# First feed-forward product of an encoder block with seven block products instead of eight, in six of eight groups

## The chip, the cores and the metric

One Trainium2 chip, of which the kernel uses 1 core. The metric is the device time of one launch in microseconds (us). Engines: TensorE (PE), VectorE (DVE), ScalarE (ACT), GpSimd (POOL) and SyncE (SP, which here only issues DMAs).

## What is computed

One layer of a residual block on x (1024 tokens x 1024, float32). What comes ahead of the feed-forward part (projections, chunked retention, stick-breaking attention, merge, output projection) is not touched. The feed-forward part is:

```
h2 = modulate(rmsnorm(h_res, pre_ffn_g), sh2, sc2)        # 1024 x 1024
f  = square(relu(h2 @ w_ff1)) @ w_ff2                     # w_ff1: 1024 x 4096, w_ff2: 4096 x 1024
h_res = h_res + gt2 * rmsnorm(f, post_ffn_g)
```

## The kernel before, in words

**Precision.** Every large product is made of two-part operands: a value is rounded to the PE's float32 format (`_hi`) and the rest is kept as a second part (`_lo`). A product is three matmuls into one PSUM bank (high by high, high by low, low by high): the triples at L549 to L551 and L933 to L935. ACT (sometimes DVE or POOL) makes the high part, DVE or POOL the low part.

**Groups.** The 4096 hidden columns are taken in 8 groups of 512 (`FF_G`). In each group PE first computes the hidden tiles, h2 times 512 columns of `w_ff1`, transposed: 8 tiles of 128 columns x 512 tokens (`ff_hidden`, 8 x 8 row chunks x 3 = 192 matmuls of 128x512). ACT takes ReLU and square of each tile into `hid` (L1259, L1261). Then comes the second product, `hid` times 512 rows of `w_ff2`, which is added to y. It is already a 2x2 block scheme with seven block products (P1, P4, P6, P5, P7, P3, P2 in the order of work, 7 x 24 = 168 matmuls, `product`); sums of the blocks a11, a12, a21, a22 of `hid` are made on DVE (L1782 to L1799), those of the blocks b11 to b22 of `w_ff2` on POOL (`add`, L487), the high parts on ACT (`w_high` L1248, `f_high` L1275), the low parts on DVE (`f_low`, L1763) and POOL (`low`, L487). DVE adds each finished bank into y (`evict`, L1776). Group 7 (`ff_last`) has no block scheme in its second product: 16 tiles x 12 matmuls (L975 to L977), with the final normalisation and the output rows behind each pair of tiles.

**Banks.** PSUM has eight banks: `pg` is banks 0 to 3, `px` banks 4 to 7. Hidden tiles use `pg` in turn; P1, P6, P7, P2 use `px`, the other three `pg`.

**Order.** Each engine runs one list of instructions in order and waits on semaphores; the order is written out by hand. Group 0 is unrolled, groups 1 to 6 are one loop, group 7 is unrolled. SP loads the weights in units of 512 KB, each when its buffer is free: four units of `w_ff1` through `raw` (2 slots), four of `w_ff2` into `w2`. The split token operands h2 stay in SBUF as `r_hi` and `r_lo` (64 KB a partition together) for all eight groups. Rounded weights have four slots in `w_hi` and `w_lo`.

Of the kernel before, what the change touches and what calls it, by code (L numbers as in the profile page):

```python
# [8 lines left out]
P = 128  # L9
D = 1024  # L10
# [120 lines left out]

class Steps:
# [19 lines left out]
def build_block(nc, x, wstream, ada, ada_rows, smalls, pos, ident, maskd, dprime, adab, postg, out, m1_dram, mods, x2_dram):  # L152
# [4 lines left out]
    with ctx:  # L157
# [86 lines left out]
        with ExitStack() as c:  # L244
            rh_f = sb("rh_f", [P, KC, S], f32, c)
            rl_f = sb("rl_f", [P, KC, S], f32, c)
# [7 lines left out]
        b11, b12, b21, b22 = (w2[:, b, :] for b in range(4))  # L254
        s2, t4 = hs[:, :, :], hs[:, :, :].rearrange("p a n -> p (a n)")
# [83 lines left out]
        gtg2_ready = sem("gtg2_ready")  # L339
        block = ctx.enter_context(nc.Block())  # L340
# [5 lines left out]
        def _(sp):  # L346
# [96 lines left out]
        def _(pool):  # L443
# [50 lines left out]
            def ff_group(g):  # L494
                first = isinstance(g, int)
                low(g, 4 + P1, 0, b11)
                pool.wait_ge(w2_in[1], 16 * g + 16)
                pool.wait_ge(ff_wlo, FF_UNITS * g + 4 + P1 + 1)
                add(b11, b12, b11, ALU.subtract).then_inc(ff_t, 1)
                if first:  # L500
# [4 lines left out]
                if not first:  # L505
# [1430 lines left out]
```

## Time and profile before

| | |
|---|---|
| time, median of 3 runs | 1748.8 us (1746.43 to 1750.7) |
| the profiled execution's own time | 1748.63 us |
| its span | 1746.8 us |
| mean granted TensorE clock | 0.995 |
| busy: PE, DVE, ACT, POOL | 1710.7, 904.0, 561.0, 603.5 us |
| moved by DMA over the span | 135.16 MB, mean 77 GB/s |

Busy time of PE counts matmuls whose ends are modelled, and one matmul's record overlaps the next. A row of a timeline gives start and duration; what stands in brackets is the idle time of the engine before it and what ended it. The share of the clock is the granted one, 1.00 being 2.4 GHz and 0.50 being 1.2 GHz.

### The profile page before, as it was taken

The page shows a single profiled execution, that of the slowest core. Times are in us where ns is not written, and L with a number is a line of the kernel's source. Part 1 is how long each engine was busy: PE and PEld are TensorE (multiplying, and loading weights), DVE is VectorE, ACT ScalarE, POOL GpSimd, SP SyncE. Part 2 cuts the span into 40 slices and gives each one's busy share as a digit, 9 for nine tenths or more (in the row PEclk, how much of TensorE's full clock was granted, in tenths as well). Part 3 has the DMA queues.
Part 4 walks back from the last instruction along what each step waited for, and adds up shares of the span by engine and source line. Part 5 has one row for each costly group of instructions (what it writes and reads, how often), then busy time and mean ns, then how long its engine had stood idle before and what let it go on. Part 6 is the DMA issues. An engine that isn't in the chain of part 4 may idle for free.

```text
span 1746.8 us, 25538 instructions
## 1 busy us (share of the span) xinstructions
PE 1710.7 (98%) x10016; PEld 1424.9 (82%) x10016; DVE 904.0 (52%) x1285; ACT 561.0 (32%) x952; POOL 603.5 (35%) x256
## 2 busy tenths in 40 slices
PE   5999999999999999999999999999999999999998
PEld 5877877777989898988888998788888888888876
DVE  6757676776446555652112277726261726252526
ACT  4556666210121212120002166333333333323242
POOL 1012111353323323233333742653535354444420
PEclk8999999999999999999999999999999999999999
DMA  8001001264401010113111545111111202020213
GB/s 341 25 25 50 17 33 61 85 217 169 148 25 52 25 53 31 46 37 133 48 48 48 175 164 193 48 49 51 46 60 36 72 24 72 24 85 12 71 66 127
DMA packets 38303, 135.16 MB, mean 77 GB/s; under 512 B 5956, under 2 KB 6852, under 8 KB 37704
## 3 DMA queue, kind: packets, MB, share of 16 engines
q1 hardware_dynamic: 30384, 109.66, 18.1%
q10 hardware_dynamic: 7832, 24.28, 3.7%
q8 instruction: 62, 1.02, 0.2%
q14 instruction: 25, 0.20, 0.0%
HBM read 121.33 MB, written 12.60 MB: 77 GB/s over the span
## 4 chain that ended last, share of the span: by engine, by line
PE 91%; DVE 4%; ACT 1%; DMA 1%; issue 1%; SPq 1%; POOL 0%; POOLq 0%; DVEq 0%; ACTq 0%
PE ps L551 17%; PE ps L549 17%; PE ps L550 17%; PE ps L933 5%; PE ps L935 5%; PE ps L934 5%; PE ps L636 3%; PE ps L637 3%; PE ps L638 3%; PE ps L812 2%; PE ps L689 2%; PE ps L814 2%; PE ps L813 2%; PE ps L653 1%; PE ps L671 1%; DMA ada_s<-ada 1%
## 5 line engine op out<-in xcount | busy, mean ns | idle before, releaser
L451 POOL TENSOR_TENSOR w_hi<-raw,zero 128x1024 fp32r<-128x1024 f32 x58 | 113.4, 1955 | 463.8 <-PE ps L551 279.9
L551 PE MATMUL ps<-r_hi,w_lo 128*128 128x512 f32 x640 | 254.3, 397 | 0.0
L549 PE MATMUL ps<-r_hi,w_hi 128*128 128x512 f32 x640 | 252.3, 394 | 0.0
L550 PE MATMUL ps<-r_lo,w_hi 128*128 128x512 f32 x640 | 252.0, 394 | 0.0
L549 PE MATMUL ps<-w_hi,a_hi 128*128 128x256 f32 x768 | 219.2, 285 | 0.8 <-DVE a_lo L1660 0.6
L551 PE MATMUL ps<-w_hi,a_lo 128*128 128x256 f32 x768 | 215.6, 281 | 0.0
L550 PE MATMUL ps<-w_lo,a_hi 128*128 128x256 f32 x768 | 215.3, 280 | 0.0
L487 POOL TENSOR_TENSOR w_lo<-w,w_hi 128x1024 fp32r<-128x1024 f32 x39 | 100.1, 2568 | 213.8 <-ACT w_hi L1248 213.8
L1776 DVE TENSOR_TENSOR m<-m,ps 128x512 f32<-128x512 f32 x208 | 136.6, 684 | 72.0 <-PE ps L935 71.5
L933 PE MATMUL ps<-w_hi,f_hi 128*128 128x512 f32 x392 | 155.5, 397 | 0.4 <-issue 0.4
L935 PE MATMUL ps<-w_hi,f_lo 128*128 128x512 f32 x392 | 155.4, 396 | 0.0
L934 PE MATMUL ps<-w_lo,f_hi 128*128 128x512 f32 x392 | 155.4, 396 | 0.0
L453 POOL TENSOR_TENSOR w_lo<-raw,w_hi 128x1024 fp32r<-128x1024 f32 x58 | 145.2, 2503 | 4.6
L549 PEld LDWEIGHTS ps<-w_hi,a_hi 128*128 128x128 f32 x768 | 144.8, 189 | 2.3 <-issue 0.9
L550 PEld LDWEIGHTS ps<-w_lo,a_hi 128*128 128x128 f32 x768 | 144.9, 189 | 0.2
L550 PEld LDWEIGHTS ps<-r_lo,w_hi 128*128 128x128 f32 x640 | 120.1, 188 | 30.3
L551 PEld LDWEIGHTS ps<-w_hi,a_lo 128*128 128x128 f32 x768 | 144.6, 188 | 0.0
L549 PEld LDWEIGHTS ps<-r_hi,w_hi 128*128 128x128 f32 x640 | 120.1, 188 | 28.9 <-DVE r_lo L1707 0.5
L551 PEld LDWEIGHTS ps<-r_hi,w_lo 128*128 128x128 f32 x640 | 120.1, 188 | 28.5
L1476 DVE TENSOR_TENSOR_SCAN uu<-uu 128x512 f32<-128x512 f32 (+7 forms) x96 | 96.1, 1041 | 77.3 <-ACT uu L1078 77.1
L1763 DVE TENSOR_TENSOR f_lo<-hid,f_hi 128x1024 fp32r<-128x1024 f32 x35 | 51.5, 1472 | 149.7 <-ACT f_hi L1275 149.7
L464 POOL TENSOR_TENSOR w_lo<-raw,w_hi 128x1024 fp32r<-128x1024 f32 x16 | 42.8, 2679 | 233.1 <-ACT w_hi L1000 205.2
(244 smaller groups left out, 3436.1 us busy)
## 6 DMA issues: line engine op xcount, KB each, us to landing
raw<-wstream SPq DMA_DIRECT2D x112, 512.0 KB, 3.6
ada_r<-ada_rows SPq DMA_DIRECT2D x32, 512.0 KB, 4.5
w<-wstream SPq DMA_DIRECT2D x32, 512.0 KB, 3.6
ada_s<-ada SPq DMA_DIRECT2D x7, 1024.0 KB, 17.1
m_dram<-m1s ACTq DMA_DIRECT2D x1, 4096.0 KB, 15.9
m<-m_dram ACTq DMA_DIRECT2D x1, 4096.0 KB, 13.0
x_dram<-m ACTq DMA_DIRECT2D x8, 512.0 KB, 5.1
rl_f<-x_dram ACTq DMA_DIRECT2D x2, 2048.0 KB, 9.4
```

What stands on the lines that cost most here:

```text
L451: nc.gpsimd.tensor_tensor(w_hi[:, slot, part], raw[:, h, :], zero[:, 0:1].broadcast_to([P, RAW]), ALU.add).then_inc(w_split, 1)
L453: nc.gpsimd.tensor_tensor(w_lo[:, slot, part], raw[:, h, :], w_hi[:, slot, part].bitcast(f32), ALU.subtract).then_inc(w_split, 1)
L487: return nc.gpsimd.tensor_tensor(out_, in0, in1, op)
L549: nc.tensor.matmul(outp, lh, rh, start=(k == 0), stop=False)
L550: nc.tensor.matmul(outp, lh, rl, start=False, stop=False)
L551: last = nc.tensor.matmul(outp, ll, rh, start=False, stop=(k == chunks - 1))
L636: nc.tensor.matmul(outp, hi, r_hi_, start=start, stop=False)
L933: nc.tensor.matmul(banks[:, t, :], fh, wh, start=(start and c == 0), stop=False, skip_group_check=not start)
L934: nc.tensor.matmul(banks[:, t, :], fh, wl, start=False, stop=False, skip_group_check=not start)
L935: last = nc.tensor.matmul(banks[:, t, :], fl, wh, start=False, stop=(c == 1), skip_group_check=not start)
L1476: V.tensor_tensor_scan(run, run, run, 1.0, ALU.mult, ALU.bypass).then_inc(scan_done, 1)
L1776: V.tensor_tensor(dst, dst, bank, op).then_inc(ff_ev, 1)
```

## The change

From the third group on (`FF_PLAIN = 2`) the hidden phase is a 2x2 block scheme as well. The blocks are the two halves of the 1024 rows of `w_ff1` (the sum's direction), the two halves of the tokens, and the two halves of the group's 512 columns. Seven products (Q1, Q2, Q6, Q7, Q5, Q4, Q3 in the order of work) of 2 banks x 4 chunks x 3 = 24 matmuls each take the place of 8 tiles of 24.

- The moving operands are seven: three are blocks of h2 (R11, R12, R22), four are sums of blocks (S1 to S4). They are the same in every group. SP stores the three in group 0 (6 DMAs of 1 MB). In group 1, DVE makes the four sums row block by row block (`operand_sums(k)`, k = 0 to 3, 13 instructions of 128x512 each), ACT rounds them (`sums_high(k)`, 4 instructions each), and SP stores both parts (16 DMAs of 512 KB). They go through slots 1 and 2 of `f_hi` and `f_lo`; a block's sums wait for the stores of the block before, and ACT's `f_high` of P4 and P6 waits for the last stores.
- `r_hi` and `r_lo` make room for a ring of three slots of 2 MB (`ring`) and four buffers for `w_ff1` (`w1s`). SP loads an operand into a slot as soon as the product that used the slot is done: seven loads of 2 MB per group.
- POOL makes the four sums of blocks of `w_ff1` and 7 low parts instead of 4; ACT makes 7 high parts instead of 4. With the second product this is 14 weight units a group instead of 11.
- The banks hold running sums: Q1, Q6 and Q7 accumulate in the same two banks, and ACT copies these out after each of the three (6 copies a group, `copied`); DVE adds the other banks to these copies in `hid` (8 additions, `h_sum`). Only then ACT takes ReLU and square, in place.
- The order of the second product stays. Group 1 is unrolled, groups 2 to 6 are the loop, group 7 takes its token tiles in the order 4 to 7, 0 to 3 (`LAST_T`) and loads the residual rows (`rl_f`) earlier.

The core of the diff:

```diff
+FF_PLAIN = 2
+Q1, Q2, Q6, Q7, Q5, Q4, Q3 = range(7)
+O_R11, O_R12, O_S2, O_S3, O_S1, O_R22, O_S4 = range(7)
+Q_WSLOT = (0, 1, 2, 3, 0, 1, 2)
+Q_RING = (0, 1, 2, 0, 1, 2, 0)
+P_WSLOT_W = (3, 0, 1, 2, 3, 0, 2)
+F_FREE_W = (8, 0, 4, 12, 16, 20, 24)
+W_UNITS, W_TILES, W_COPIES, W_ADDS, FF2_TILES = 14, 14, 6, 8, 28
+TL_W = TL_FF + FF_PLAIN * FF_TILES
+LAST_T = (4, 5, 6, 7, 0, 1, 2, 3)
...
+            ring = sb("ring", [P, 3, 2, 4, HALF], f32r, c)
+            w1s = sb("w1s", [P, 4, RAW], f32, c)
...
+            sp.wait_ge(n2_split, 32)
+            for o, k, th in ((O_R11, 0, 0), (O_R12, 4, 0), (O_R22, 4, 1)):
+                for part, a in enumerate((r_hi, r_lo)):
+                    sp.dma_start(ops[o, :, part, :, :], a[:, k:k + 4, th * HALF:(th + 1) * HALF].bitcast(f32)).then_inc(r_out, 16)
...
+            for k in range(4):
+                for pair, lo_done, to in ((0, 11, ops[O_S2:O_S3 + 1]), (1, 13, ops[O_S1:O_S4 + 1:2])):
+                    sp.wait_ge(s_val, 13 * k + lo_done)
+                    for part, f in enumerate((f_hi, f_lo)):
+                        sp.dma_start(to[:, :, part, k, :].rearrange("s p n -> p s n"), f[:, 1 + pair, :, :].bitcast(f32)).then_inc(s_out[pair], 16)
...
+            for o in range(3):
+                ring_load(o, gemm_done, TL_FF + FF_TILES + 8)
...
+            with sp.Fori(FF_PLAIN, FF_G - 1) as g:
+                wu = w_unit(g)
+                sp.wait_ge(w1_t, 4 * (g - FF_PLAIN) + 1)
+                w1_load(g + 1, 0, ff_wlo, wu + Q1 + 1)
+                ring_load(3, *h_done(g, 0))
+                ring_load(4, *h_done(g, 1))
+                ring_load(5, *h_done(g, 2))
+                w1_load(g + 1, 1, ff_wlo, wu + Q7 + 1)
+                ring_load(6, *h_done(g, 3))
+                ring_load(1, *h_done(g, 4))
+                w1_load(g + 1, 2, ff_wlo, wu + Q4 + 1)
+                ring_load(2, *h_done(g, 5))
+                ring_load(0, *h_done(g, 6))
+                w1_load(g + 1, 3, ff_wlo, wu + Q3 + 1)
...
+            def hidden_ahead(g, done):
+                n = 4 * (g - FF_PLAIN)
+                pool.wait_ge(ff_wlo, done)
+                if not isinstance(g, int) or g > FF_PLAIN:
+                    pool.wait_ge(w1_t, n)
+                for b in range(2):
+                    pool.wait_ge(w1_in[b], 16 * (g - 1))
+                add(u1, v12, v11, ALU.subtract).then_inc(w1_t, 1)
+                pool.wait_ge(w1_in[3], 16 * (g - 1))
+                pool.wait_ge(w1_t, n + 1)
+                add(u2, v22, u1, ALU.subtract).then_inc(w1_t, 1)
+                w_low(g, Q1, Q_WSLOT[Q1], v11)
+                w_low(g, Q2, Q_WSLOT[Q2], v21)
+            def hidden_units(g):
+                n = 4 * (g - FF_PLAIN)
+                w_low(g, Q6, Q_WSLOT[Q6], u2)
+                add(v12, v22, v12, ALU.subtract).then_inc(w1_t, 1)
+                w_low(g, Q7, Q_WSLOT[Q7], v12)
+                w_low(g, Q5, Q_WSLOT[Q5], u1)
+                pool.wait_ge(ff_wlo, w_unit(g) + Q2 + 1)
+                pool.wait_ge(w1_t, n + 2)
+                add(v21, u2, v21, ALU.subtract).then_inc(w1_t, 1)
+                w_low(g, Q4, Q_WSLOT[Q4], v21)
+                w_low(g, Q3, Q_WSLOT[Q3], v22)
...
+            def w_group(g):
+                wu = w_unit(g)
+                hidden_units(g)
+                w_low(g, 7 + P1, P_WSLOT_W[P1], b11)
+                second_sums(g, wu + 7 + P1 + 1)
+                w_low(g, 7 + P4, P_WSLOT_W[P4], t4)
+                w_low(g, 7 + P6, P_WSLOT_W[P6], t2)
+                w_low(g, 7 + P5, P_WSLOT_W[P5], b11)
...
+            def hidden_product(g, q, banks, start, free):
+                turn, slot = g - FF_PLAIN, Q_RING[q]
+                pe.wait_ge(ff_wlo, w_unit(g) + q + 1)
+                pe.wait_ge(ring_in[slot], (48 if slot == 0 else 32) * turn + 16 * (q // 3 + 1))
+                for m in range(2):
+                    pe.wait_ge(*free(m))
+                    for k in range(4):
+                        wh, wl = (w[:, Q_WSLOT[q], k * 256 + m * P:k * 256 + (m + 1) * P] for w in (w_hi4, w_lo4))
+                        xh, xl = (ring[:, slot, part, k, :] for part in range(2))
+                        nc.tensor.matmul(banks[:, m, :], wh, xh, start=(start and k == 0), stop=False, skip_group_check=not start)
+                        nc.tensor.matmul(banks[:, m, :], wl, xh, start=False, stop=False, skip_group_check=not start)
+                        last = nc.tensor.matmul(banks[:, m, :], wh, xl, start=False, stop=(k == 3), skip_group_check=not start)
+                    last.then_inc(h_mm, 1)
+            def hidden_products(g):
+                turn, ev = g - FF_PLAIN, FF_EVS * (g - 1)
+                x_banks, z_banks, y_banks, w_banks = px[:, 0:2, :], px[:, 2:4, :], pg[:, 0:2, :], pg[:, 2:4, :]
+                hidden_product(g, Q1, x_banks, True, lambda m: (ff_ev, ev + E_P2 + m + 1))
+                hidden_product(g, Q2, z_banks, True, lambda m: (ff_ev, ev + E_P2 + m + 3))
+                hidden_product(g, Q6, x_banks, False, lambda m: (h_copy, W_COPIES * turn + m + 1))
+                hidden_product(g, Q7, x_banks, False, lambda m: (h_copy, W_COPIES * turn + m + 3))
+                hidden_product(g, Q5, y_banks, True, lambda m: (ff_ev, ev + E_P3 + m + 1))
+                hidden_product(g, Q4, w_banks, True, lambda m: (ff_ev, ev + E_P3 + m + 3))
+                hidden_product(g, Q3, y_banks, False, lambda m: (h_add, W_ADDS * turn + m + 3))
...
+            def sums_high(k):
+                for n, ready in ((1, 3), (0, 5), (2, 8), (3, 9)):
+                    act.wait_ge(s_val, 13 * k + ready)
+                    nc.scalar.activation(f_hi[:, 1 + n // 2, n % 2, :], sum_slot(n), ACT.Copy).then_inc(s_hi, 1)
...
+                    if j == 0 and not first:
+                        sums_high(0)
...
+                    if j == 2 and not first:
+                        sums_high(1)
...
+                    sums_high(2)
...
+                    sums_high(3)
...
+                else:
+                    act.wait_ge(s_out[0], 16 * 8)
...
+                else:
+                    act.wait_ge(s_out[1], 16 * 8)
...
+            def hidden_part(g, seconds):
+                turn, tl, t1 = g - FF_PLAIN, w_tiles(g), 4 * (g - FF_PLAIN)
+                def h(q):
+                    return h_mm, W_TILES * turn + 2 * q + 2
+                act.wait_ge(ff_lo, FF_PRODS * g)
+                unit_high(Q_WSLOT[Q6], u2, (gemm_done, tl + 8), (w1_t, t1 + 2))
+                copied(g, 0, 0, 0, px[:, 0, :])
+                unit_high(Q_WSLOT[Q7], v12, (gemm_done, tl), (w1_t, t1 + 3))
+                copied(g, 1, 1, 0, px[:, 1, :])
+                unit_high(Q_WSLOT[Q5], u1, h(Q1), (w1_t, t1 + 1))
+                squared(g, 0, 0, 0)
+                squared(g, 1, 1, 0)
+                f_high_w(g, P1, a11, ff_sq, 8 * g + 2)
+                unit_high(Q_WSLOT[Q4], v21, h(Q2), (w1_t, t1 + 4))
+                copied(g, 2, 2, 0, px[:, 0, :])
+                copied(g, 3, 3, 0, px[:, 1, :])
+                unit_high(Q_WSLOT[Q3], v22, h(Q6), (w1_in[3], 16 * (g - 1)))
+                copied(g, 4, 0, 1, px[:, 0, :])
+                copied(g, 5, 1, 1, px[:, 1, :])
+                unit_high(*seconds[0])
+                squared(g, 2, 2, 1)
+                squared(g, 3, 3, 1)
+                unit_high(*seconds[1])
+                f_high_w(g, P4, a22, ff_sq, 8 * g + 4)
+                squared(g, 4, 0, 1)
+                squared(g, 5, 1, 1)
+                unit_high(*seconds[2])
...
+            def operand_sums(k):
+                def s_(f, n):
+                    return f[:, 1 + n // 2, n % 2, :]
+                def step(n, out_, in0, in1, op, after):
+                    if after:
+                        dve.wait_ge(s_val, 13 * k + after)
+                    V.tensor_tensor(out_, in0, in1, op).then_inc(s_val, 1)
+                (h11, l11), (h21, l21), (h12, l12), (h22, l22) = (
+                    tuple(r[:, c, th * HALF:(th + 1) * HALF].bitcast(f32) for r in (r_hi, r_lo))
+                    for c, th in ((k, 0), (k, 1), (4 + k, 0), (4 + k, 1)))
+                x2_, x3, x1, x4 = (sum_slot(n) for n in range(4))
+                tmp = fs_f[:, 1, HALF:D]
+                if k:
+                    dve.wait_ge(s_out[0], 32 * k)
+                else:
+                    dve.wait_ge(gemm_done, TL_FF + 28)
+                step(1, x3, h11, h21, ALU.subtract, 0)
+                step(2, tmp, l11, l21, ALU.subtract, 0)
+                step(3, x3, x3, tmp, ALU.add, 2)
+                step(4, x2_, h22, x3, ALU.subtract, 3)
+                step(5, x2_, x2_, l22, ALU.add, 4)
+                if k:
+                    dve.wait_ge(s_out[1], 32 * k)
+                else:
+                    dve.wait_ge(gemm_done, TL_FF + 32)
+                step(6, x1, x2_, h11, ALU.add, 5)
+                step(7, x4, h12, x2_, ALU.subtract, 0)
+                step(8, x1, x1, l11, ALU.add, 6)
+                step(9, x4, x4, l12, ALU.add, 7)
+                for m, n in enumerate((1, 0, 2, 3)):
+                    dve.wait_ge(s_hi, 4 * k + m + 1)
+                    step(10 + m, s_(f_lo, n), sum_slot(n), s_(f_hi, n).bitcast(f32), ALU.subtract, 9 if m == 0 else 0)
...
+                    for k in range(3):
+                        operand_sums(k)
...
+                else:
+                    operand_sums(3)
...
+            def hidden_sums(g):
+                for m in range(2):
+                    h_sum(g, m, half(m, 0), half(m, 0), px[:, 2 + m, :], ALU.add, 1 + m)
+                f_low_w(g, 0, 0, a11)
+                for m in range(2):
+                    h_sum(g, 2 + m, half(2 + m, 1), half(m, 1), pg[:, m, :], ALU.add, 5 + m)
+                f_low_w(g, 1, 1, a22)
+                for m in range(2):
+                    h_sum(g, 4 + m, half(m, 1), half(m, 1), pg[:, 2 + m, :], ALU.subtract, 5 + m)
```

## Rows read from the trace of the kernel before

**Rows 1.** The page: busy time, and shares of the chain that ended last.
```profile
PE 1710.7 (98%) x10016; PEld 1424.9 (82%) x10016; DVE 904.0 (52%) x1285; ACT 561.0 (32%) x952; POOL 603.5 (35%) x256
...
PE 91%; DVE 4%; ACT 1%; DMA 1%; issue 1%; SPq 1%; POOL 0%; POOLq 0%; DVEq 0%; ACTq 0%
```

**Rows 2.** The waits of PE: total us, times, longest (first and seventh of 12).
```profile
PE ps L601 <- DMA ada_s<-ada: 17.9, 1, 17.9
...
PE ps L975 <- POOL w_lo L487: 0.7, 1, 0.7
```

**Rows 3.** Groups by line on PE: busy us, mean ns.
```profile
L551 PE MATMUL ps<-r_hi,w_lo 128*128 128x512 f32 x640 | 254.3, 397 | 0.0
L549 PE MATMUL ps<-r_hi,w_hi 128*128 128x512 f32 x640 | 252.3, 394 | 0.0
```

**Rows 4.** Timeline of PE: first matmul of group 1 and of group 2.
```profile
1144.07 0.39 PE L549 MATMUL ps<-r_hi,w_hi 128*128 128x512 f32 x1
...
1228.21 0.40 PE L549 MATMUL ps<-r_hi,w_hi 128*128 128x512 f32 x1
```

**Rows 5.** Window of group 1's hidden phase: busy PE, PEld, DVE, ACT, POOL; clock, DMA, GB/s.
```profile
1144.00:1189.00 45.00, 45.00 (x194) 36.20 (x194) 10.07 (x7) 16.77 (x22) 22.50 (x9) 1.00 0.09 33
```

**Rows 6.** DVE on two SBUF tensors (line L1652): min/median/max ns.
```profile
L1652 DVE TENSOR_TENSOR m<-m,gate x16: 691/693/2841, 812.8 to 962.3; 128x512 f32 x12, 128x512 f32<-128x512 f32 x4
```

**Rows 7.** DMA issues: KB each, us to landing; whole span, and three short windows.
```profile
w<-wstream SPq DMA_DIRECT2D x32, 512.0 KB, 3.6
...
x_dram<-m ACTq DMA_DIRECT2D x8, 512.0 KB, 5.1
...
x_dram<-m ACTq DMA_DIRECT2D x1, 512.0 KB, 9.1
...
rl_f<-x_dram ACTq DMA_DIRECT2D x1, 2048.0 KB, 7.2
...
rl_f<-x_dram ACTq DMA_DIRECT2D x2, 2048.0 KB, 9.4
```

**Rows 8.** Timeline of DVE and of POOL in group 1, the same stretch.
```profile
1169.05 2.08 DVE L1763 TENSOR_TENSOR f_lo<-hid,f_hi 128x1024 fp32r<-128x1024 f32 x1 [24.10 <-ACT f_hi L1275]
1171.05 3.41 DVE L1782 TENSOR_TENSOR hid<-hid 128x1024 f32<-128x1024 f32 x1
...
1167.63 2.42 POOL L487 TENSOR_TENSOR w<-w 128x1024 f32<-128x1024 f32 x1
1170.04 3.34 POOL L487 TENSOR_TENSOR w_lo<-hs,w_hi 128x1024 fp32r<-128x1024 f32 x1
```

**Rows 9.** Groups by line on ACT from 1140 on: busy us, mean ns.
```profile
L1248 ACT ACTIVATE w_hi<-w 128x1024 fp32r<-128x1024 f32 x34 | 35.5, 1044 | 0.0
L1261 ACT ACTIVATE hid<-hid 128x512 f32<-128x512 f32 x56 | 35.4, 633 | 1.8
L1259 ACT ACTIVATE hid<-ps 128x512 f32<-128x512 f32 x56 | 33.5, 598 | 186.1 <-PE ps L551 186.1
```

**Rows 10.** Timeline of DVE: the low part of a22 in group 1.
```profile
1186.10 1.22 DVE L1763 TENSOR_TENSOR f_lo<-hid,f_hi 128x1024 fp32r<-128x1024 f32 x1
```

**Rows 11.** Windows around PE's stop of 1.9 us; the clock is third from last.
```profile
96.00:97.00 1.00, 0.00 (x0) 0.00 (x0) 0.05 (x1) 1.00 (x4) 1.00 (x1) 1.00 0.00 0
...
98.00:99.00 1.00, 1.00 (x4) 0.75 (x4) 0.79 (x3) 0.00 (x0) 0.00 (x0) 0.64 0.35 70
99.00:100.00 1.00, 1.00 (x4) 0.81 (x3) 0.00 (x0) 0.00 (x0) 0.00 (x0) 0.50 0.85 279
100.00:101.00 1.00, 1.00 (x3) 0.72 (x3) 0.00 (x0) 0.00 (x0) 0.00 (x0) 0.50 0.42 168
101.00:102.00 1.00, 1.00 (x4) 0.84 (x3) 0.00 (x0) 0.00 (x0) 0.00 (x0) 0.65 0.02 8
```

**Rows 12.** Window while two loads of 2048 KB are under way; GB/s is last.
```profile
1703.00:1705.00 2.00, 2.00 (x10) 1.58 (x10) 1.71 (x3) 0.00 (x0) 0.00 (x0) 1.00 1.07 459
```

More of the change, by code:

```diff
@@ new lines, in _, with w1_load, ring_load @@
+            for c in range(2):
+                load(unit(1, c), c, (ff_wlo, 2 + c + 1))
+            for b, p in ((0, P5), (1, P7), (3, P3), (2, P2)):
+                ff_second(1, b, (ff_wlo, 4 + p + 1))
+            for c in range(2, 4):
+                load(unit(1, c), c - 2, (ff_wlo, FF_UNITS + c - 1))
+            def w1_load(g, b, *after):
+                sp.wait_ge(*after)
+                sp.dma_start(w1[b], unit(g, b)).then_inc(w1_in[b], 16)
+            def ring_load(o, *after):
+                sp.wait_ge(*after)
+                sp.dma_start(ring[:, Q_RING[o], :, :, :].bitcast(f32), ops[o, :, :, :, :]).then_inc(ring_in[Q_RING[o]], 16)
@@ L922, in ff_hidden, with passes_t, product @@
                             h2_transposed(u)
-            def product(g, i, banks, start, free):
-                pe.wait_ge(ff_wlo, FF_UNITS * g + 4 + i + 1)
+            def passes_t(bank, hidden, weight, start, stop, skip):
+                (fh, fl), (wh, wl) = hidden, weight
+                nc.tensor.matmul(bank, fh, wh, start=start, stop=False, skip_group_check=skip)
+                nc.tensor.matmul(bank, fh, wl, start=False, stop=False, skip_group_check=skip)
+                return nc.tensor.matmul(bank, fl, wh, start=False, stop=stop, skip_group_check=skip)
+            def product(g, i, banks, start, free, unit, slot):
+                pe.wait_ge(ff_wlo, unit + i + 1)
                 pe.wait_ge(ff_lo, FF_PRODS * g + i + 1)
@@ new lines, in unit_high, with hidden_ahead @@
+            def unit_high(slot, src, free, ready):
+                act.wait_ge(*ready)
+                act.wait_ge(*free)
+                nc.scalar.activation(w_hi4[:, slot, :], src, ACT.Copy).then_inc(ff_whi, 1)
+            def hidden_ahead(g):
+                end = w_tiles(g) + 8
+                unit_high(Q_WSLOT[Q1], v11, (gemm_done, end - 4), (w1_in[0], 16 * (g - 1)))
+                unit_high(Q_WSLOT[Q2], v21, (gemm_done, end - 4 if isinstance(g, int) else end - 16), (w1_in[2], 16 * (g - 1)))
@@ L1776, in evict @@
                     V.tensor_tensor(dst, dst, bank, op).then_inc(ff_ev, 1)
+                if not first:
+                    for k in range(3):
+                        operand_sums(k)
                 f_low(P1, a11)
@@ L1817, in ff_group, with h_sum @@
                 dve.wait_ge(ff_ev, ev + FF_EVS)
[L1819 to L1824 removed]
+            def h_sum(g, n, dst, src, bank, op, copy):
+                turn = g - FF_PLAIN
+                dve.wait_ge(h_mm, W_TILES * turn + (3, 4, 9, 10, 11, 12, 13, 14)[n])
+                dve.wait_ge(h_copy, W_COPIES * turn + copy)
+                V.tensor_tensor(dst, src, bank, op).then_inc(h_add, 1)
```

372 lines of the change are left out of this document (248 added, 124 removed).

## The prediction, made before the changed kernel was built or run

> **What bounds the kernel now.** I read the page first. TensorE (PE) is busy 98% of the span and makes 91% of the chain that ended last [rows 1]. The list of its waits says the same: the one long wait is for the first inputs, and within the feed-forward stage only the last group shows one, 0.7 us [rows 2]. So in the groups that the change touches, PE never waits, and the stage costs its matmuls. A matmul's printed duration (394 to 397 ns, the same at each of the three places of a triple) is no price, since they overlap [rows 3]. The price is the distance of starts: the first matmul of group 1 starts at 1144.07 and that of group 2 at 1228.21, with 360 matmuls of 128x512 between them, so one costs 84.14/360 = 0.2337 us [rows 4]. 24 of them, now one hidden tile and in the new scheme one product, cost 5.61 us. DVE is busy 10.1 us of the 45 of group 1's hidden phase, ACT 16.8 and POOL 22.5 [rows 5]; all three have room, and the question is whether the change fills it in the wrong place.
>
> **What is removed.** In groups 2 to 7 the hidden phase goes from 8 tiles x 24 = 192 matmuls to 7 products x 24 = 168. The bound engine loses 24 x 0.2337 = 5.61 us per group, 33.7 us for six. The order inside a triple becomes high-high, low-high, high-low; I cost it at nothing, because the three places have the same mean today. Everything else the change does is added work, which costs nothing while it lies beside PE.
>
> **Added once: the operands, in group 1.** Six stores of 1 MB of the token operands go out on SP's queue at the end of the split in group 0. Behind them on SP wait only loads for group 1, needed a group later: nothing. Then DVE makes four sums for each of four row blocks, 13 steps of 128x512 each, 52 in all, ACT rounds 16 of them, and 16 stores take them to DRAM. These are a chain. A block's step 1 overwrites what the block before is still storing, so it waits for that block's first pair of stores, issued after step 11. And DVE stands in order: the low part of a11 (needed by P1) is behind block 2, the low part of a22 (needed by P4) behind block 3 and, through ACT, behind block 3's stores.
> Prices: a DVE step between SBUF tensors lasts 0.69 us, some 0.65 per step where they follow closely, so 11 steps 7.2 us [rows 6]. A 512 KB store has landed after 5.1 us, and a pair after some 5.5 us with the second issue [rows 7]. DVE and POOL hold each other up: DVE's low part started at 1169.05 and took 2.08 us, and the next operation 3.41, while POOL's operations ran 1167.63 to 1170.05 and then 3.34 us instead of 2.42; the two take turns [rows 8].
> In time from the group's first matmul: ACT can round only after ReLU and square of the first tile, 5.61 + 1.23 = 6.9 [rows 9], and the first block's step 11 is over at about 12.4. Its stores have landed at 17.9. Block 1 takes 7.2 plus three POOL operations that come between (weight sums and lows, 3 x 2.4): 32.3. Stores 37.8; block 2 to 45.0; two steps and the low part of a11 to 47.4, while P1 wants it at 8 x 5.61 = 44.9. Block 2's stores 50.5; block 3 to 57.7; its stores 63.2; ACT's copy 64.3; the low part of a22 at 65.5. P4 wants it at 50.5 (today it is there at 1187.3, 43.2 after the start [rows 10]). That is 15.0 us late, and 1 us more while evictions catch up: **16 us**. Bounds: 1 us, if blocks never hold P4 (DVE has 35 idle us in this phase); 30 us, if each of the four store pairs takes the 9.1 us that one store took in a busy moment.
> After a stop of 1.9 us (PE has no instruction from 96 to 97) the granted clock stood at 0.64, 0.50, 0.50 and 0.65 for the next four microseconds, that is at the lower of the two levels (1.2 GHz) for most of it: 1.7 us lost [rows 11]. I add 1.7 for the long stop; bounds 0 and 3.4 (two stops).
>
> **Added in every group from 2 on.** ACT gets 6 copies from PSUM and 3 weight roundings (about 6.5 us), DVE 8 additions with a PSUM operand (5.5 us), POOL 7 operations (17 us) [rows 6, 8, 9]. Against a group of 336 x 0.2337 = 78.5 us that is room enough, so only order matters. I laid the steps against products of 5.61 us. Weights of Q6 high, low 3.5; POOL's sum 5.9; Q7 high 7.0, low 9.4; Q5 low 11.8; the next sum 14.3; ACT, in order, rounds Q4's weights to 15.3 and only then copies Q6's first bank, 15.9; Q7 wants that bank at 16.8: 0.9 us to spare. Further on POOL's four sums end at 36.3, DVE's low part of a22 stands behind them, then sums, ReLU, square and the evictions of P1: P4 has 1.5 us to spare, P6 some 1.9, and P5's first bank 0.4 us. No stop, but margins of under a microsecond; I take 0.1 us per group, bounds 0 and 2.5. In the last group the low part of a21 is about 1.0 us late, while the wait of 0.7 us there today goes, since its weights have 4.2 us of matmuls over them and need 3.6 [rows 2]: +0.3. Together 0.8 us.
> The ring: seven loads of 2 MB per group, on SP. A load is issued when its slot's product ends and is wanted two products, 11.2 us, later. A 2048 KB load of the same shape landed after 7.2 us, the second issued 0.4 us behind it after 11.7 (the median of both is 9.4), so 4.9 us each when they follow [rows 7]. Four such loads and one of 0.5 MB (8.9 MB) are wanted between the end of Q1 and the start of Q3, with 25.8 us for the transfers: 346 GB/s. A window of a loaded queue shows 459 GB/s [rows 12]. So the ring holds with about 4 us to spare: nothing. The Trainium skill (DMA: Bandwidth & Descriptors, Specifications) gives an HBM limit near 358 GB/s per core; by that the spare would be 0.9 us and the sum the same. By the 341 GB/s that its section Bandwidth gives for 1 MB each group would stop 0.3 us and the sum be 2 us more. This trace's window stands above both figures.
>
> **Sum**, against the profiled execution's own time of 1748.6 (span 1746.8; the median of three runs is 1748.8): 1748.6 - 33.7 + 16.0 + 1.7 + 0.8 = **1733.4 us**. The 0.2 between that execution and the median is left aside.
>
> **Rivals.**
> B, group 1 hides its sums, and nearly all of the saving is kept. For it: DVE is idle 35 of 45 us there, and ACT 28. Against: the chain of four blocks and stores above is 57 us long and has only 50.5. 1748.6 - 33.7 + 1 + 0.8 = 1716.7.
> C, the groups of the loop stop as well, in P5's or Q7's bank wait: each margin is under 1 us, and one more blocked POOL operation (3.34 - 2.42 = 0.9 us, [rows 8]) in each of two chains eats it. 2.5 us per loop group, five of them: 1733.4 + 12.5 = 1745.9, from 1737 to 1750.
> D, the other side: **slower**, by the ring. If loads on the queue do not overlap and each takes its 7.2 us [rows 7], then four of them and the 512 KB load (3.6 us) end at 5.6 + 32.4 = 38.0 and Q3, which wants the last at 33.7, stops 4.3 to 5 us in each group: 1733.4 + 6 x 4.7 = 1761.6. It decides from about 6.9 us per load. Against: the two loads that did overlap.
> E, the products save nothing, since weights of 256 columns and the ring as moving operand cost more per matmul: 1733.4 + 33.7 = 1767.1. Against: rows 3, one price for all operands.
>
> **Chances.** Forecast 0.60, B 0.15, C 0.14, D 0.07, E 0.04. A measurement of this kernel can tell about 0.2%, 3.5 us, from no change. Forecast and B are faster, and of C two thirds (below 1745.3): faster 0.84. The rest of C and the upper end of the forecast: same 0.07. D and E: slower 0.09 with rounding. The range takes in B's 1716 below, and above the group-1 bound and most of C, 1748; D and E are left out.
>
> **What would show it.** Right: PE's waits in the profile of after name DVE's low part for the first matmul of P4, once, with 10 to 15 us, and of P1 with about 2; group 1 takes about 100 us instead of 84.1, each loop group 78.5 to 79; the granted clock falls once, behind that stop. Wrong: no such wait (B); waits for evictions or ACT's copies five times over (C); waits for the DMA into the ring (D); a start distance above 0.234 us in the products (E).

## The result, and the profile after

The changed kernel takes 1759.4 us (median of four runs, 1756.1 to 1766.1) against 1749.8 for the kernel before beside it: the ratio is 1.0064, with a 95% interval of 1.0047 to 1.0082. It is slower by 0.6%. The prediction had said 1733.4 us, between 1716 and 1748, and faster with a chance of 0.84. It was wrong in its sign.

The page of the changed kernel begins with the busy times; the profiled execution took 1756.1 us:

```profile
span 1754.3 us, 25638 instructions
...
PE 1686.2 (96%) x9872; PEld 1401.3 (80%) x9872; DVE 995.2 (57%) x1385; ACT 606.4 (35%) x1022; POOL 711.5 (41%) x298
...
PE 70%; POOL 10%; issue 9%; DVE 5%; ACT 3%; DMA 2%; SPq 0%; DVEq 0%; POOLq 0%; ACTq 0%
```

Beside [rows 1] TensorE's (PE's) share falls from 98% to 96% of a longer span, and in the chain that ended last from 91% to 70%. Ten per cent of that chain are now GpSimd (POOL), five VectorE (DVE). PE does less work and waits for others. Its waits, with the total, the number and the longest in us:

```profile
PE ps L1074 <- DVE m L2193: 14.0, 5, 2.8
PE ps L1074 <- issue: 14.0, 4, 7.9
PE ps L1074 <- DVE hid L2163: 4.7, 5, 1.0
```

The kernel before had none of these ([rows 2]). Two of them come five times, once in each group of the loop (groups 2 to 6): 0.84 to 0.98 us ahead of P4's first matmul, for VectorE's last hidden sums, and 2.8 us ahead of P5's, for VectorE's evictions of P4's banks. The two lines of "DVE" are the loop's; the line of "issue" holds the stops of 2.65 and 7.88 us in group 1, the last group's of 3.04, and one of 0.39 that the kernel before has too. The timeline of PE shows the loop's and the two stops of group 1; a row has start, duration, line, operation, and in brackets the idle time before it and what ended it:

```profile
1189.13 0.77 PE L1074 MATMUL ps<-w_hi,f_hi 128*128 128x512 f32 x1 [2.65 <-issue]
...
1205.64 0.77 PE L1074 MATMUL ps<-w_hi,f_hi 128*128 128x512 f32 x1 [7.88 <-issue]
...
1286.85 0.51 PE L1074 MATMUL ps<-w_hi,f_hi 128*128 128x512 f32 x1 [0.84 <-DVE hid L2163]
...
1301.15 0.80 PE L1074 MATMUL ps<-w_hi,f_hi 128*128 128x512 f32 x1 [2.78 <-DVE m L2193]
1301.74 0.63 PE L1075 MATMUL ps<-w_lo,f_hi 128*128 128x512 f32 x1
1302.17 0.63 PE L1076 MATMUL ps<-w_hi,f_lo 128*128 128x512 f32 x1
```

The last two rows start 0.43 us apart in place of 0.23: that is the lower clock level (1.2 GHz) behind a stop. By stage, with the window, its length, the busy time and count of PE, PEld, DVE, ACT and POOL, then the granted clock, the DMA share and GB/s. The rows are group 1's hidden and second products, group 2's, group 4's, and the last group's hidden products:

```profile
1141.51:1189.13 47.62, 44.97 (x194) 35.88 (x192) 39.70 (x41) 20.41 (x30) 21.05 (x8) 0.99 0.35 128
1189.13:1240.95 51.82, 43.94 (x168) 34.92 (x169) 42.70 (x54) 16.95 (x21) 22.80 (x9) 0.87 0.65 255
1240.95:1280.24 39.29, 39.29 (x169) 31.45 (x168) 7.15 (x9) 18.59 (x25) 32.03 (x14) 1.00 0.84 337
1280.24:1325.24 45.00, 41.38 (x170) 32.65 (x168) 38.46 (x42) 15.59 (x19) 23.32 (x10) 0.96 0.33 127
1409.62:1448.82 39.20, 39.20 (x170) 31.53 (x168) 7.15 (x9) 18.43 (x25) 31.84 (x14) 1.00 0.84 333
1448.82:1492.48 43.66, 39.87 (x169) 31.48 (x168) 37.69 (x42) 15.73 (x19) 23.50 (x10) 1.00 0.35 132
1659.68:1702.09 42.41, 39.37 (x169) 31.38 (x168) 11.07 (x11) 22.65 (x30) 25.49 (x12) 1.00 0.60 229
```

What the reader is to see:
- Group 1 takes 47.62 + 51.82 = 99.4 us in place of 84.1 [rows 4]: +15.3.
- The seven hidden products take 39.2 us, 0.2333 us per matmul, with PE busy all the time while the ring is loaded at 337 GB/s. That stage saves its 5.6 us in full.
- The second products behind them take 43.7 to 45.0 us, where 168 matmuls without a stop need 39.3. The saving goes there: loop groups take 82.8 to 84.4 us, 83.7 in the mean (418.7 us from 1240.95 to 1659.68 for five), against 84.1 before.
- The last group stops for 3.04 us ahead of its second products.
- A stop costs more than the time in its brackets: the brackets count from the end of the last matmul's record, 0.39 us long, where the next would have started after 0.23, and the first start behind a stop is followed late. Experiment 1 gives the price of one alone: 1.2 us for 0.98 in brackets.

Over the whole span, from 1746.8 to 1754.3 us: group 1 begins 2.6 us earlier here than in the profile of before, and takes 15.3 more; the five loop groups take 418.7 - 5 x 84.14 = -2.0; what is left behind them takes 94.6 in place of 1746.8 - (1228.21 + 5 x 84.14) = 97.9, so -3.3. The sum is +7.4.

### The profile page after: what moved, and what is told of

The parts are those of the page before. It is cut to its first block, busy times and chain, and to the rows that moved or that the text cites. A ratio compares the mean times of both kernels' runs of the same rounds, so it can differ in the third digit from the quotient of the medians.

```text
span 1754.3 us, 25638 instructions
## 1 busy us (share of the span) xinstructions
PE 1686.2 (96%) x9872; PEld 1401.3 (80%) x9872; DVE 995.2 (57%) x1385; ACT 606.4 (35%) x1022; POOL 711.5 (41%) x298
## 4 chain that ended last, share of the span: by engine, by line
PE 70%; POOL 10%; issue 9%; DVE 5%; ACT 3%; DMA 2%; SPq 0%; DVEq 0%; POOLq 0%; ACTq 0%
PE ps L696 12%; PE ps L698 11%; PE ps L697 11%; POOL w_lo L578 5%; PE ps L1074 3%; PE ps L1075 3%; PE ps L1076 3%; PE ps L783 3%; PE ps L784 3%; PE ps L785 3%; PE ps L959 2%; POOL w1s L578 2%; PE ps L836 2%; PE ps L961 2%; PE ps L960 2%
## 5 line engine op out<-in xcount | busy, mean ns | idle before, releaser
L1074 PE MATMUL ps<-w_hi,f_hi 128*128 128x512 f32 x440 | 179.7, 408 | 32.7 <-DVE m L2193 14.0
L1075 PE MATMUL ps<-w_lo,f_hi 128*128 128x512 f32 x440 | 178.0, 405 | 0.0
L1076 PE MATMUL ps<-w_hi,f_lo 128*128 128x512 f32 x440 | 177.5, 403 | 0.0
L1119 PE MATMUL ps<-ring,w_hi 128*128 128x512 f32 x336 | 133.1, 396 | 0.0
L1117 PE MATMUL ps<-ring,w_hi 128*128 128x512 f32 x336 | 132.7, 395 | 0.0
L1118 PE MATMUL ps<-ring,w_lo 128*128 128x512 f32 x336 | 132.5, 394 | 0.0
L1074 PEld LDWEIGHTS ps<-w_hi,f_hi 128*128 128x128 f32 x440 | 85.2, 194 | 59.1 <-DVE m L2193 16.2
L2193 DVE TENSOR_TENSOR m<-m,ps 128x512 f32<-128x512 f32 x160 | 99.9, 678 | 15.0 <-PE ps L1076 14.3
L2163 DVE TENSOR_TENSOR hid<-hid,ps 128x512 f32<-128x512 f32 x48 | 31.8, 681 | 129.4 <-PE ps L1119 129.4
L1076 PEld LDWEIGHTS ps<-w_hi,f_lo 128*128 128x128 f32 x440 | 85.2, 194 | 21.0
L696 PE MATMUL ps<-r_hi,w_hi 128*128 128x512 f32 x256 | 101.9, 398 | 0.1
```

The source lines that it names most:

```text
L696: nc.tensor.matmul(outp, lh, rh, start=(k == 0), stop=False)
L1074: nc.tensor.matmul(bank, fh, wh, start=start, stop=False, skip_group_check=skip)
L1075: nc.tensor.matmul(bank, fh, wl, start=False, stop=False, skip_group_check=skip)
L1076: return nc.tensor.matmul(bank, fl, wh, start=False, stop=stop, skip_group_check=skip)
L1117: nc.tensor.matmul(banks[:, m, :], wh, xh, start=(start and k == 0), stop=False, skip_group_check=not start)
L1118: nc.tensor.matmul(banks[:, m, :], wl, xh, start=False, stop=False, skip_group_check=not start)
```

## Why VectorE was late: the theory before the runs

The timeline of VectorE in group 2's second products:

```profile
1281.64 1.22 DVE L2197 TENSOR_TENSOR hid<-hid 128x1024 f32<-128x1024 f32 x1 [1.95 <-ACT hid L1556]
1282.90 3.30 DVE L2200 TENSOR_TENSOR hs<-hid 128x1024 f32<-128x1024 f32 x1
1286.12 1.27 DVE L2163 TENSOR_TENSOR hid<-hid,ps 128x512 f32<-128x512 f32 x2
...
1291.39 2.48 DVE L2193 TENSOR_TENSOR m<-m,ps 128x512 f32<-128x512 f32 x4
1293.78 3.40 DVE L2208 TENSOR_TENSOR hs<-hid,hs 128x1024 f32<-128x1024 f32 x1
1297.11 3.38 DVE L2172 TENSOR_TENSOR f_lo<-hid,f_hi 128x1024 fp32r<-128x1024 f32 x1
1300.42 2.47 DVE L2193 TENSOR_TENSOR m<-m,ps 128x512 f32<-128x512 f32 x4
```

and of GpSimd in the same stretch:

```profile
1282.64 2.48 POOL L578 TENSOR_TENSOR w_lo<-gate,w_hi 128x1024 fp32r<-128x1024 f32 x1 [1.86 <-ACT w_hi L1535]
1291.29 8.12 POOL L578 TENSOR_TENSOR w_lo<-w,w_hi 128x1024 fp32r<-128x1024 f32 x3 [6.17 <-ACT w_hi L1535]
```

A VectorE operation of 128x1024 between SBUF operands takes 1.22 us when it is left alone. Three here take 3.3 to 3.4, each beside a GpSimd operation (a "meeting" in what follows). L2200 became ready 0.26 us after GpSimd had begun the low part of P6's weights (1282.64); the sums that free P4's banks (L2163) stand behind it, and P4 stopped. In the same way L2208 and L2172 each lost 2.2 us to the second and third low part of GpSimd's row of three (P5's, P7's, P3's); the evictions that free P5's first banks stand behind them, and P5 stopped for 2.8 us. The evictions themselves, with an operand in PSUM, kept their 0.62 us each beside the first. L2200, L2208 and the L2172 behind it take 3.29 to 3.43 us in every group of the loop. P7's and P3's weights are wanted only 5.6 and 11.2 us after P5's.

So **the theory**: GpSimd's low parts, made earlier than needed, take VectorE's turns on SBUF. The Trainium skill (SBUF — State Buffer, Who interferes with whom) says that such a pair of operations goes by an exclusive lock held for a whole instruction, and that the issue order decides who blocks. The rows agree: the 3.40 us of L2208 are 2.2 of waiting behind a GpSimd operation that had begun and the 1.22 of its own.

**Rivals**: VectorE's list alone is too long, whoever runs beside it; ScalarE's high parts, which moved with GpSimd's, are in the way; the ring's loads slow the others. For group 1 the theory is the forecast's chain of sums and stores. The page names only "issue" for its two stops, but VectorE's low parts of a11 and of a22 end just ahead of the two rows of PE above, at 1189.03 (PE: 1189.13) and 1205.55 (1205.64):

```profile
1187.81 1.22 DVE L2097 TENSOR_TENSOR f_lo<-hid,f_hi 128x1024 fp32r<-128x1024 f32 x1
...
1204.32 1.23 DVE L2097 TENSOR_TENSOR f_lo<-hid,f_hi 128x1024 fp32r<-128x1024 f32 x1 [1.64 <-ACT f_hi L1478]
```

## The experiments

All ratios are against the kernel before, on the same chip in the same batch. "Less than the changed kernel" compares medians of different batches, in which the kernel before took 1749.8 (changed kernel), 1749.3 (experiments 1, 3, 4 and 5) and 1748.5 us (2, 6 and 7); differences of one or two microseconds in it say nothing.

**1. GpSimd's low parts of P7 and P3 later.**

```diff
-                unit_high(*second(P7, b12, (gemm_done, tl + 12), ff_t, 4 * g + 4))
+                unit_high(*second(P7, b12, (gemm_done, tl + 18), ff_t, 4 * g + 4))
...
-                unit_high(*second(P3, b22, (gemm_done, tl + 16), w2_in[3], 16 * g + 16))
+                unit_high(*second(P3, b22, (gemm_done, tl + 22), w2_in[3], 16 * g + 16))
```

> Only ScalarE's gates of the high parts of P7's and P3's weights move six tiles of the second products later, so that GpSimd does their low parts later; the instructions and their sizes stay the same. Theory (VectorE and GpSimd take turns on SBUF, and GpSimd's lows of P7 and P3 hold up VectorE's sum for a12 and the low part of P5's hidden operand): the stop of 2.8 us ahead of P5's first matmul goes, and the half clock behind it; the stop of 0.84 to 1.0 us ahead of P4 stays. Loop groups 79.5 to 80.7 us instead of 83.7, in all 15 to 22 us less than the changed kernel: about 1739 us. Rival (VectorE has too much to do between P1 and P5, whatever GpSimd does): P5's stop stays at 2.8 us, and the time at 1757 to 1760. Rival (the ring's loads hold the matmuls up): no change either.

Measured: 1739.7 us, ratio 0.9953 (0.9936 to 0.9970), 19.7 us less than the changed kernel. The waits of PE in the feed-forward stage:

```profile
PE ps L1074 <- issue: 15.5, 4, 9.1
PE ps L1074 <- DVE hid L2163: 4.8, 5, 1.0
```

The five stops of 2.8 us are gone, and the clock falls in no loop group; each takes 79.8 us (39.2 and 40.6), as expected; the five together take 398.9 in place of 418.7. P4's stop stays, as the theory said. It is now alone in its stage, so its price can be read: 0.98 us in brackets, and 40.59 us against the 39.35 of a stage without a stop.

```profile
1282.40:1322.99 40.59, 39.61 (x169) 31.56 (x168) 34.56 (x42) 15.85 (x19) 23.33 (x10) 1.00 0.38 143
```

Two numbers in two lines of ScalarE's list turn the change from a loss into a gain.

**2. GpSimd alone later.** The first experiment moved ScalarE's work too. Here ScalarE keeps its times.

```diff
+                pool.wait_ge(gemm_done, w_tiles(g) + 18)
                 w_low(g, 7 + P7, P_WSLOT_W[P7], b12)
+                pool.wait_ge(gemm_done, w_tiles(g) + 22)
                 w_low(g, 7 + P3, P_WSLOT_W[P3], b22)
```

> As in the first experiment, but ScalarE keeps its times: only GpSimd waits, ahead of its lows of P7 and P3, for the tiles of the second products that ScalarE waited for there. Theory (it is GpSimd's turns on SBUF that hold VectorE up): the stop of 2.8 us ahead of P5 goes as in the first experiment, loop groups 79.8 us, time 1738 to 1742 us. Rival (the moved work of ScalarE was the cause, its high parts in VectorE's way): the stop stays, 1755 us or more.

Measured: 1740.3 us, ratio 0.9951 (0.9939 to 0.9964), the same as the first. VectorE's timeline at the same place of group 2:

```profile
1293.90 2.47 DVE L2195 TENSOR_TENSOR m<-m,ps 128x512 f32<-128x512 f32 x4
1296.29 1.22 DVE L2210 TENSOR_TENSOR hs<-hid,hs 128x1024 f32<-128x1024 f32 x1
1297.42 1.22 DVE L2174 TENSOR_TENSOR f_lo<-hid,f_hi 128x1024 fp32r<-128x1024 f32 x1
1298.56 2.47 DVE L2195 TENSOR_TENSOR m<-m,ps 128x512 f32<-128x512 f32 x4
```

The same instructions in the same order; the two behind the first evictions take 1.22 us in place of 3.40 and 3.38. For P5's stop, VectorE's list is not too long and ScalarE is not the cause: it is GpSimd's turns.

**3. The hidden sums first.** VectorE makes the sums that free P4's banks ahead of the two subtractions.

```diff
                 hidden_sums(g)
+                for m in range(2):
+                    h_sum(g, 6 + m, half(2 + m, 0), half(2 + m, 0), pg[:, m, :], ALU.add, 3 + m)
                 dve.wait_ge(ff_sq, 8 * g + 6)
...
-                for m in range(2):
-                    h_sum(g, 6 + m, half(2 + m, 0), half(2 + m, 0), pg[:, m, :], ALU.add, 3 + m)
                 f_low_w(g, P6, P_FSLOT[P6], s2)
```

> Only VectorE's order changes: the last two sums of the hidden tile (numbers 6 and 7, which free P4's banks) come ahead of the two subtractions that form a11 - a21 and s2. Theory: the stop of 0.84 to 1.0 us ahead of P4 goes in each of the five loop groups, and the stop ahead of P5 shrinks by up to 0.8 us because VectorE's list shifts; 4 to 9 us less than the changed kernel, about 1752 us. Rival (work amount of VectorE alone sets both stops): the 0.9 us only moves to P5's stop, time as before this edit, 1757 to 1760.

Measured: 1752.7 us, ratio 1.0019 (1.0006 to 1.0031), 6.8 us less than the changed kernel, within the 4 to 9 expected. In the profile the loop's five groups take 408.7 us in place of 418.7.

```profile
PE ps L1074 <- issue: 15.5, 4, 9.1
PE ps L1074 <- DVE m L2193: 11.8, 5, 2.4
```

P4's stop is gone and P5's fell from 2.8 to 2.4 us. The 0.9 us did not move on to P5: the rival of pure work amount fails here as well. That P4's stop itself comes from a meeting is worked out and not tested: L2200 loses 2.1 us to GpSimd's low part of P6's weights, more than the stop of 0.84 to 0.98, but no run took that meeting away. What this run shows is that the order of VectorE's list decides.

**4. Both orders, and the last group's.** To both edits comes one in the last group: ScalarE makes the high part of a21 ahead of the third weight unit's.

```diff
                 squared(g, 5, 1, 1)
+                if isinstance(g, int):
+                    act.wait_ge(ff_sq, 8 * g + 6)
+                    act.wait_ge(gemm_done, w_tiles(g) + 4)
+                    nc.scalar.activation(f_hi[:, 2, :, :], a21, ACT.Copy).then_inc(ff_hi, 1)
                 unit_high(*seconds[2])
```

> Both edits together, and in the last group ScalarE makes the high part of a21 ahead of the high part of the third weight unit. Theory: no stop over 0.3 us in any loop group, each 78.5 to 79 us; the last group's stop of 3.0 us falls to 1 us or less; group 1 stays at 99.4 us. In all 25 to 29 us less than the changed kernel: about 1731 us, that is 18 us below the kernel before. Rival (work amount): loop groups stay above 82 us and the time above 1752 us.

Measured: 1731.0 us, ratio 0.9902 (0.9885 to 0.9919), 28.4 us less than the changed kernel. By stage: group 1's second products, group 2's hidden and second products, the last group's hidden products:

```profile
1191.23:1243.95 52.72, 43.59 (x169) 34.59 (x170) 43.60 (x54) 16.95 (x21) 22.90 (x9) 0.87 0.64 250
1243.95:1283.15 39.20, 39.20 (x169) 31.55 (x168) 7.57 (x10) 18.43 (x25) 31.93 (x14) 1.00 0.85 338
1283.15:1322.51 39.36, 39.36 (x169) 31.65 (x168) 34.73 (x42) 15.86 (x19) 23.33 (x10) 1.00 0.39 146
1636.69:1676.98 40.29, 39.37 (x169) 31.38 (x168) 9.76 (x11) 22.23 (x30) 22.32 (x11) 1.00 0.58 217
```

A loop group is 39.20 + 39.36 = 78.6 us, 336 matmuls at 0.234: PE without a stop, and the full 5.6 us saved in each. The last group's stop is 0.9 us; with either order alone it was still 3.0 (experiments 1 and 3), so it is the third edit that shortened it. VectorE's subtraction that forms s2 is still blocked (3.31 us); the sums that P4 waits for no longer stand behind it, so it costs nothing.

**5. No operand sums.** Left out: the 52 operand sums of group 1 with their 16 high parts and 16 stores; the ring's four slots of sums are filled from operands that are in DRAM anyway.

```diff
-                    for k in range(3):
-                        operand_sums(k)
...
-                    operand_sums(3)
...
-                sp.dma_start(ring[:, Q_RING[o], :, :, :].bitcast(f32), ops[o, :, :, :, :]).then_inc(ring_in[Q_RING[o]], 16)
+                sp.dma_start(ring[:, Q_RING[o], :, :, :].bitcast(f32), ops[(O_R11, O_R12, O_R11, O_R22, O_R12, O_R22, O_R11)[o], :, :, :, :]).then_inc(ring_in[Q_RING[o]], 16)
```

> Left out: the 52 operand sums of group 1 with their ScalarE high parts and their 16 stores; the ring's four slots of sums are filled from three operands that are in DRAM anyway, so traffic and matmuls stay the same. Theory: group 1's stops of 2.65 and 7.9 us and the half clock behind each go, group 1 falls from 99.4 to 84.1 us, everything behind stays: 15 to 16 us less than the changed kernel, about 1744 us. Rival (the stops of group 1 come from loads or from GpSimd's own work): group 1 stays above 92 us, time above 1751 us.

Measured: 1747.3 us, ratio 0.9986 (0.9974 to 0.9997). Group 1, hidden and second products:

```profile
1148.30:1193.10 44.80, 44.80 (x194) 36.04 (x193) 10.58 (x7) 16.77 (x22) 22.50 (x9) 1.00 0.09 32
1193.10:1232.44 39.34, 39.34 (x169) 31.64 (x168) 26.79 (x37) 11.28 (x12) 20.26 (x8) 1.00 0.61 243
```

44.80 + 39.34 = 84.1 us without a stop: the sums and stores are all of group 1's 15.3, and the rival falls. The time is a miss: the median fell by 12.2 us and not by 15 to 16. Between the two profiled executions it is 8.5, that is 15.3 less in group 1 and 6.8 more ahead of it, where no instruction was edited (group 1 begins at 1148.30 here and at 1141.51 in the changed kernel's). The loop's groups keep their stops and their 418.7 us.

**6. The ring's traffic.** Left out: nearly all bytes of the loop's ring loads (16 partitions by 16 columns of each row in place of 2 MB); waits and counts are kept.

```diff
-                sp.dma_start(ring[:, Q_RING[o], :, :, :].bitcast(f32), ops[o, :, :, :, :]).then_inc(ring_in[Q_RING[o]], 16)
+                sp.dma_start(ring[0:16, Q_RING[o], :, :, 0:16].bitcast(f32), ops[o, 0:16, :, :, 0:16]).then_inc(ring_in[Q_RING[o]], 16)
```

> Left out: nearly all of the ring's traffic. In the loop each of the seven loads into the ring moves 16 partitions by 16 columns of each row in place of 2 MB, so 35 loads of 2 MB go; the matmuls read what the ring held before, waits and counts are the same. Theory: the ring's loads cost nothing in the changed kernel, since the hidden stage runs at 0.2333 us per matmul with no stop: the time stays at 1757 to 1761 us. Rival (the loads' traffic slows VectorE and GpSimd in SBUF or lengthens the weights' landings, and so makes the stops): loop groups below 82 us and the time below 1750 us.

Measured: 1762.5 us, ratio 1.0079 (1.0065 to 1.0092), 3 us above the changed kernel and 1.5 above the bound given. Its waits:

```profile
PE ps L1079 <- issue: 16.8, 4, 10.7
PE ps L1079 <- DVE m L2198: 14.0, 5, 2.8
PE ps L1079 <- DVE hid L2168: 5.0, 5, 1.0
```

The loop's stops are what they were with 35 loads of 2 MB beside them, and its five groups take 419.0 us against 418.7 (1245.98 to 1664.93). The ring costs nothing. It was close, though. In the changed kernel's group 2 a load takes up to 10.9 us from its issue to its landing (first row: minimum, median, maximum), where 11.2 are allowed: the one issued at 1263.54 was there at 1274.43, and Q3, which reads it, began at 1274.55. For 25 us the loads moved 396 GB/s at a DMA share of 0.98 (second row):

```profile
DMA to landing us min/median/max: 8.4/10.2/10.9
```

```profile
1249.00:1274.40 25.40, 25.40 (x111) 20.34 (x109) 3.98 (x5) 11.99 (x17) 20.18 (x9) 1.00 0.98 396
```

Whether the 3 us are more than noise is open (the intervals of the two ratios overlap); they are not in the loop. The two profiled executions lie 8.1 us apart: 4.1 ahead of group 1; 1.0 in group 1's second products (52.8 us against 51.8), which were not edited; 0.2 in the loop; and 2.8 behind the last group's stop, where the clock falls, which it didn't in the changed kernel (26.8 us against 24.0 for the next 102 matmuls).

**7. The sums in two groups.** On top of experiment 4, group 2 keeps eight products as well, the seven begin in group 3, and the four blocks of sums are made two in group 1 and two in group 2; the loads, counts and gates of group 2 follow those of group 1.

```diff
-FF_PLAIN = 2
+FF_PLAIN = 3
...
-                    for k in range(3):
+                    for k in (2 * g - 2, 2 * g - 1):
                         operand_sums(k)
...
-                    operand_sums(3)
```

> On top of both orders: group 2 too keeps its eight products, the seven products begin in group 3, and the operand sums are made half in group 1 and half in group 2. It gives up 24 matmuls (5.6 us) and should be rid of group 1's stops (99.4 us against 84.1 us without the sums). Theory (only the length of VectorE's list ahead of the low part of a11 and of a22 makes these stops, and two blocks are done some 33 us into a group, 15 us ahead of P1): groups 1 and 2 take 84.1 to 84.5 us each, the loop groups 78.6 us, in all 9 to 10 us less than with both orders in place: about 1721 us, 28 us below the kernel before. Rival (the stops come with the sums wherever they stand, in proportion): groups 1 and 2 take some 91 us each and the time is 1735 us or more.

Measured: 1725.1 us, ratio 0.9850 (0.9834 to 0.9866). It is 1.5% faster than the kernel before. By stage: group 1, group 2, then the first group with seven products:

```profile
1148.80:1193.60 44.80, 44.80 (x194) 36.04 (x193) 38.86 (x33) 21.33 (x30) 23.77 (x9) 1.00 0.35 126
1193.60:1232.94 39.34, 39.34 (x169) 31.64 (x168) 27.05 (x37) 11.39 (x12) 15.24 (x6) 1.00 0.22 72
1232.94:1277.74 44.80, 44.80 (x193) 36.04 (x192) 38.73 (x33) 21.33 (x30) 23.26 (x9) 1.00 0.35 125
1277.74:1317.09 39.35, 39.35 (x169) 31.64 (x168) 27.24 (x37) 11.28 (x12) 20.30 (x8) 1.00 0.61 243
1317.09:1356.29 39.20, 39.20 (x170) 31.54 (x168) 7.57 (x10) 18.47 (x25) 31.93 (x14) 1.00 0.86 341
1356.29:1395.64 39.35, 39.35 (x170) 31.64 (x168) 34.70 (x42) 15.85 (x19) 23.30 (x10) 1.00 0.39 143
```

VectorE is busy 38.9 of 44.8 us in the hidden phase, nearly as in the changed kernel (39.7), and PE does not stop once in groups 1 to 6: the same sums are free where only two blocks stand ahead of the low part of a11. The second block is done 34.1 us into the group, 10.7 ahead of P1 (the expectation's 15 was not right). The size came out 4 us short of the expected 1721: two of the five runs took 1720, three 1725 to 1726, and in the profiled one, of the latter three, group 1 begins 5.2 us later than in experiment 4. From there to the end it takes 575.5 us against 586.1, so 10.6 less where 9 to 10 were expected.

## Why the prediction was wrong, step by step

- **The removed matmuls, 33.7 us: right.** Per group 5.61 us; experiment 4 shows 84.14 - 78.56 = 5.6 in each loop group. Rival E falls.
- **The ring, nothing: right.** No wait for it in any profile, 39.2 us per hidden stage at 337 GB/s, and none of the stops went with the traffic in experiment 6. But the spare was not the 4 us of the forecast. The last load that group 2 needed was there 0.1 us before Q3 began (experiment 6), so the term came out right by little. Rival D, the only one on the slower side beside E, falls, though the kernel is slower.
- **Group 1, 16.0 and 1.7 us: right.** Sum 17.7, measured 15.3, shown by experiment 5 (15.3 to 16.3 in the six profiles that have all sums in group 1). The forecast had the low part of a22 at 65.5 us after the group's start; it came at 1204.32 + 1.23 - 1141.51 = 64.0. The third block's stores were forecast at 45.0 and issued at 45.2 (1186.71). The stops are 2.65 and 7.9 us where 2 and 10 to 15 were named. P4's first matmul came 64.1 us after the start, 13.6 later than the 50.5 at which it was wanted, where 15.0 were forecast; another 1.7 us went behind it, where 1.0 and 1.7 had been set. Nineteen matmuls ran at the lower clock (3.7 us), but 13 of them between the two stops, where P4 waited for VectorE anyhow. The clock fell behind both stops and again in the loop, not once. Rival B falls.
- **A price inside that chain was short.** Six steps of the first two blocks met a GpSimd operation and took 2.8 to 2.9 us in place of 0.69, four of them in the second block (8.5 us, where the forecast set 7.2 for three GpSimd operations). How much of group 1's 15.3 us would go if GpSimd's weight sums stood elsewhere was not tried.
- **The loop groups: the step that failed.** "No stop, but margins of under a microsecond; I take 0.1 us per group, bounds 0 and 2.5" was 5.2 us per group (83.7 - 78.5), 26 us in all. It is nearly the whole miss. In the profiled execution, 1756.1 us, the parts are: 25.5 more in the loop (26 where 0.5 was set), 2.4 less in group 1, 2.0 more in the last group (0.3 forecast, 2.3 measured: 3.04 in place of 0.7), and 2.6 less ahead of group 1, so 1733.4 + 22.5 = 1755.9. That 1733.4 + 26 also gives the median, 1759.4, is chance.
- **What was wrong inside that step.** The step let VectorE's operations take their free time and named no GpSimd low part beside them on the way to P4 and P5. Rival C had the sign right, waits for evictions in the five loop groups, but its price of 2.5 came from one blocked GpSimd operation (0.9 us) in each of two chains. It read the turn-taking of [rows 8] from GpSimd's side. From VectorE's side the same rows say 3.41 where 1.22 is free: 2.2 us per meeting, and VectorE is the engine in the chain. Three of its operations meet one in each group, 3.30, 3.40 and 3.38 us, 6.4 us against margins of 1.5 and 0.4. The two stops make 3.7 us of the 5.2 per group visible, and cost some 0.25 us each beyond their brackets; the lower clock behind P5's adds 1.5 us in three of five groups, 0.9 in the mean.
- **The chances.** The margins of 0.4 to 1.9 us were written down beside a price per meeting of 2.2 that could be read from the rows. With margins smaller than one meeting, the loop stopping was the likely case and not one of 0.14, and its upper bound belonged at three meetings per group, above the kernel before.
- **What would show it.** The text named "waits for evictions or ACT's copies five times over" as the sign of C. That is what PE's waits show, with VectorE's hidden sums in place of ScalarE's copies. Its sign of being right, one wait for VectorE's low part of 10 to 15 us, did not come by name: the page calls group 1's stops "issue".

## What to carry to other kernels

When a change takes work from the bound engine, lay the other engines' lists against the shorter time, and price every meeting of a GpSimd operation with a VectorE operation between SBUF operands by what the VectorE one loses (here up to 2.2 us for one of 1.2), not by what GpSimd loses. Work made early is not free: two gates moved six tiles later gave 19.7 us, with no instruction changed. A one-time preparation can be worth cutting into pieces that fit beside the bound engine before their consumers stand in line, even if the new scheme starts a group later: here 5.6 us given up for some 16 us of stops.

## What the runs showed that was not expected

- **Turns, one by one.** GpSimd had three operations in a row (8.12 us) and VectorE two behind its evictions. Neither ran twice while the other waited: VectorE's 3.40 and 3.38 us are one turn of GpSimd and one of its own each, though GpSimd's operations stood ready back to back. The sums of group 1 look the same: four steps in a row of 2.8 to 2.9 us in place of 0.69, beside GpSimd's operations. How the next turn is given was not tried by itself.
- **The clock behind a stop.** After stops of equal length (2.78 to 2.81 us) at the same place of equal groups, the matmuls ran 0.43 us apart in groups 2, 3 and 5 and at full speed in groups 4 and 6 (granted clock 0.96 in the window of the first, 1.00 in that of group 4). In experiment 6 it was groups 2, 4 and 6. The price is some 1.5 us each time (45.2 against 43.7 us). Behind the last group's stop of 3.03 to 3.06 us the clock fell in experiments 2, 3 and 6 and not in the changed kernel, 1 and 5. What decides it stays open.
- **The part ahead of the edits.** Group 1 begins between 1141.5 and 1148.8 us in the profiles of the changed kernel and its variants, with the same instructions ahead of it. That range of 7.3 us is three quarters of what the whole change moves the median (9.6), so the stages and not the totals decided these experiments.
